# The last FFN's gate and up products in passes of 256 tokens instead of 512

## The reference, cut to what matters

```
h = rmsnorm_2(x, norm_ffn[l])                       # 512 tokens x 1024
x = x + (jax.nn.silu(h @ w_ffn_gate[l])             # 1024 x 2816 weights
         * (h @ w_ffn_up[l])) @ w_ffn_down[l]       # then 2816 x 1024
```

## Time and profile before

| | |
|---|---|
| median of three runs | 1888.11 us |
| profiled execution, span of the core | 1888.1 us |
| mean granted clock of TensorE | 0.998 |
| PE busy | 1859.0 us (98%) |
| PEld (weight loads) busy | 1454.0 us (77%) |
| DVE, ACT, POOL busy | 859.6, 686.3, 552.0 us |
| matmul records | 8653, as many weight loads |

### The profile page before, as it was taken

The page is one execution under the profiler, slowest core; times in us unless marked ns, Lnnn a source line. Parts: engine busy times, 40 slices in busy tenths (PEclk is TensorE's granted clock), DMA queues, the critical chain, the costliest instruction groups (busy, mean ns, idle before and its releaser), DMA issues.

```text
span 1888.1 us, 21529 instructions
## 1 busy us (share of the span) xinstructions
PE 1859.0 (98%) x8653; PEld 1454.0 (77%) x8653; DVE 859.6 (46%) x1348; ACT 686.3 (36%) x1023; POOL 552.0 (29%) x437
## 2 busy tenths in 40 slices
PE   6999999999999999999999999999999999999998
PEld 6777778877777777877888888877776788888886
DVE  6467542646261303324333333548777654423433
ACT  5555542223232323433222222435546532212223
POOL 3543344445355544431000000044556211100100
PEclk9999999999999999999999999999999999999999
DMA  9412223544343122322423322432221222222321
GB/s 300 149 50 68 68 68 123 164 147 155 120 150 110 62 74 85 130 94 87 131 79 100 112 89 70 109 95 79 87 92 58 74 90 93 90 89 91 104 87 54
DMA packets 182332, 192.46 MB, mean 102 GB/s; under 512 B 10155, under 2 KB 166065, under 8 KB 181977
## 3 DMA queue, kind: packets, MB, share of 16 engines
q1 hardware_dynamic: 179704, 180.84, 29.8%
q0 software_dynamic: 1104, 5.24, 1.0%
q10 hardware_dynamic: 1424, 5.00, 0.7%
HBM read 188.95 MB, written 4.72 MB: 103 GB/s over the span
## 4 chain that ended last, share of the span: by engine, by line
PE 93%; DVE 4%; ACT 2%; issue 1%; DMA 0%; ACTq 0%; SPq 0%; DVEq 0%
PE bank L1492 25%; PE bank L1497 24%; PE bank L1494 24%; PE bank L1517 2%; PE bank L1515 2%; PE bank L1513 2%; PE bank L1591 2%; PE bank L1525 2%; PE bank L1541 1%; PE bank L1561 1%; PE bank L1577 1%; DVE left L1859 1%; DVE ADA L1817 1%; PE bank L1471 1%; PE bank L1477 1%
## 5 line engine op out<-in xcount | busy, mean ns | idle before, releaser
L1492 PE MATMUL bank<-hH,wh 128*128 128x512 f32 x1264 | 520.4, 412 | 3.3 <-ACT hH L2221 3.0
L1497 PE MATMUL bank<-hL,wh 128*128 128x512 f32 x1264 | 501.4, 397 | 0.1
L1494 PE MATMUL bank<-hH,wl 128*128 128x512 f32 x1264 | 501.3, 397 | 0.0
L2606 POOL TENSOR_TENSOR wl<-stg,wh 128x512 fp32r<-128x512 f32 x150 | 200.0, 1333 | 792.3 <-ACT wh L2238 792.0
L2238 ACT ACTIVATE wh<-stg 128x1024 fp32r<-128x1024 f32 (+2 forms) x292 | 298.2, 1023 | 271.5 <-PE bank L1497 191.3
L1492 PEld LDWEIGHTS bank<-hH,wh 128*128 128x128 f32 x1264 | 238.4, 189 | 76.0 <-issue 23.3
L1497 PEld LDWEIGHTS bank<-hL,wh 128*128 128x128 f32 x1264 | 238.3, 189 | 58.1 <-DVE hL L1973 0.5
L1494 PEld LDWEIGHTS bank<-hH,wl 128*128 128x128 f32 x1264 | 239.1, 189 | 53.4 <-issue 2.6
L1799 DVE TENSOR_TENSOR wl<-stg,wh 128x1024 fp32r<-128x1024 f32 (+2 forms) x142 | 168.3, 1188 | 240.0 <-ACT wh L2238 239.5
L2607 POOL TENSOR_TENSOR wl<-stg,wh 128x512 fp32r<-128x512 f32 x150 | 203.8, 1359 | 0.0
L1492 PE MATMUL bank<-h2H,wh 128*128 128x512 f32 x352 | 140.6, 399 | 0.0
(11 more groups left out here) (326 smaller groups left out, 2599.8 us busy)
## 6 DMA issues: line engine op xcount, KB each, us to landing
stg<-in_w_in SPq DMA_DIRECT2D x54, 1024.0 KB, 5.1
stg<-in_w_ffn_in SPq DMA_DIRECT2D x22, 1024.0 KB, 5.1
stg<-in_w_ada SPq DMA_DIRECT2D x16, 1024.0 KB, 5.3
stg<-in_w_ffn_gate SPq DMA_DIRECT2D x11, 1024.0 KB, 5.2
stg<-in_w_ffn_up SPq DMA_DIRECT2D x11, 1024.0 KB, 5.1
stg<-in_w_ffn_down SPq DMA_DIRECT2D x10, 1024.0 KB, 5.0
stg<-in_w_ada SPq DMA_DIRECT2D x16, 512.0 KB, 6.4
stg<-in_w_proj_ret SPq DMA_DIRECT2D x8, 1024.0 KB, 5.0
```

Of the source, the lines that this page charges most:

```text
L1492: T.matmul(ps, wh, xh, start=j["first"] and k == 0, stop=False)
L1494: T.matmul(ps, wl, xh, start=False, stop=False)
L1497: t = T.matmul(ps, wh, xl, start=False, stop=j["stop"] and last)
L2606: G.tensor_tensor(lo[:, 0:h, :], src[:, 0:h, :], hi[:, 0:h, :], ALU.subtract)
```

## The change

For jobs whose activations are `h5`, each matmul over 512 tokens becomes two over 256 tokens, one behind the other, with the same weights. The first writes columns 0 to 255 of the bank, the second columns 256 to 511. The flag that starts an accumulation stands on the first half of the first matmul only; later writes accumulate. The semaphore `gemm` is raised by the second half of the last matmul. Jobs with other activations are issued as before.

```
-                T.matmul(ps, wh, xh, start=j["first"] and k == 0, stop=False)
+                last = k == j["n"] - 1
+                halves = [slice(0, S // 2), slice(S // 2, S)] if j["x"] == "h5" else [slice(0, S)]
+                for c in halves:
+                    T.matmul(ps[:, c], wh, xh[:, c], start=j["first"] and k == 0 and c.start == 0, stop=False, skip_group_check=len(halves) > 1)
                 pe.wait_ge("w_lo_" + j["lo"], j["low"])
-                T.matmul(ps, wl, xh, start=False, stop=False)
+                for c in halves:
+                    T.matmul(ps[:, c], wl, xh[:, c], start=False, stop=False, skip_group_check=len(halves) > 1)
                 low_done(pe, j["x"], j["x0"] + k)
-                last = k == j["n"] - 1
-                t = T.matmul(ps, wh, xl, start=False, stop=j["stop"] and last)
+                for c in halves:
+                    t = T.matmul(ps[:, c], wh, xl[:, c], start=False, stop=j["stop"] and last, skip_group_check=len(halves) > 1)
                 if last:
                     t.then_inc(s["gemm"], 1)
```

## The result

The change makes the kernel slower by 0.16%: the ratio to the kernel before is 1.0016, with a 95% interval from 1.0009 to 1.0023, over 17 runs of the kernel after and 16 of the kernel before (medians 1891.95 and 1889.20 us). A 17th run of the kernel before took 3698.86 us, is no fast run and is not in the ratio. The difference is clear of zero. Its middle lies within the 0.2% called no change in the prediction, and the interval's upper end just beyond. The profiled execution has a span of 1891.2 us against 1888.1, so +3.1 us, where +2.6 were forecast; the medians differ by 2.75 us.

A forecast was written before the change was run, and what follows sets the result against it. TensorE was taken to bound the kernel; 1056 pairs, each 2.5 ns dearer than one pass (237.0 against 234.5 ns), add +2.6 us to 1888.1, giving 1890.7 us. Its own range is 1888 to 1896, the wider one 1877 to 1912.

The forecast's parts named there:

- The bound: Last FFN's changed products: TensorE, busy 98% of the span, has 0.0 us idle ahead, so each ns per pass shows 1056 times.
- Twice the loads, all hidden: Each half has its own load, 1056 more in all, ready 112 ns into a 118.5 ns half, 6.5 ns to spare.
- The rival of an uncovered load or issue: Added loads or TensorE's issue of twice the instructions come into the open: up to +116 us, 2004 us; chance 0.07.
- The 21 ns as a rate: A 512-column pass's excess over 213.3 ns grows with columns, 0.453 ns a column, so a half costs 118.5 ns; chance 0.60.
- the rival of a fixed cost: Each fp32r pass keeps its 21 ns at its stream's start: 127.9 ns a half, +22.4 us, 1910.5 us; chance 0.20.
- The rival of short passes that escape: Supply runs dry only late in a stream, so halves go at the load's 112 ns: -11.1 us, 1877.0 us; chance 0.11.
- a supply of columns: In fp32r streams, the supply of columns can't keep up with 2.4 GHz; at half speed the array never waits for it.
- Cost that is there once for each pass: About 2.5 ns for each pass, read from float32 rows; an added pass per pair makes 1056 * 2.5 ns = +2.6 us.
- the sum: For a half pass: 2.5 + 256 * 0.453 = 118.5 ns, a pair 237.0 ns, 2.5 more than one whole pass.
- slower: Outcome beyond the 0.2%, 3.8 us, that a measurement tells from no change; given 0.46 in all.
- The half-clock rows: At granted clock 0.50 passes take 428 ns against 426.7 streamed: the extra is gone, where a cost in array cycles would have doubled.
- The reading that the load in the shadow takes no part of the 21 ns: Behind the pass at 1479.98, 0.227 us of stream runs with no load beside it, so the load isn't the extra's cause.

The follow-up runs named there:

- quarters: Each pass of the last FFN's gate and up products cut into four of 128 tokens, against the kernel before: 2111.64 us, ratio 1.1178.
- even and odd tokens: Changed kernel, but the first half reads even tokens and the second odd ones, 8 bytes apart; results land at wrong tokens: 2121.76 us.
- the run with ones: Kernel before, last FFN's gate and up products all bfloat16, moving operand a dense tile of ones; result left wrong: 1870.52 us.

## Why the prediction was right

The bound: right. TensorE has no idle time ahead of the halves, the stretch starts at the same 1504.2 us, and the difference is inside it.

The time: 1890.7 us were forecast and 1891.95 measured. Most of that gap is in the base and not in the change: a run's time lies 1.8 to 1.9 us above its core's span (1893.07 and 1891.2 us for the profiled run of the kernel after), so the span of 1888.1 and the first three runs' median of 1888.11 were equal by chance, and over more runs the median of the kernel before is 1889.20.

Twice the loads, all hidden: right. The load's pace, 112 ns from float32 rows, held for fp32r (111.7 in quarters), so a half has 6 to 7 ns to spare. The records are 281 to 282 ns long where 280 were forecast. The rival of an uncovered load or issue is out: TensorE was given a pass and a load every 112 ns for all of the last FFN.

The 21 ns as a rate: right in its size and wrong in what it is a rate of. The steps of 118.6 (256), 173.3 to 176.7 (384) and 234.3 (512) deny the rival of a fixed cost, which asked for 127.9 and 181.2. The rival of short passes that escape asked for 112 ns and is out by the same numbers. But "a supply of columns" was too narrow: even and odd tokens show that twice the stretch of memory for the same columns takes nearly twice the time. The prediction couldn't see that, since every moving operand of type fp32r here lies in one piece.

"Cost that is there once for each pass", 2.5 ns: this term came out near by luck, and with it the +2.6 us, which is nothing but this term. It was measured at 3.1 ns a pair in the last FFN, but it isn't a constant of a pass of fp32r: in the first FFN the same halves cost 0.4 ns a pair, and 384 columns lie on both sides of the sum's 176.5. With 117.3 ns a half the change would have cost 0.4 us. The rows didn't give the term either: a step of (1.88 - 0.59) / 3 is known to some 3 ns, and the transposes' 109 to 110 ns are also the pace of their loads, which the prediction itself puts at 110. A cost of 2.5 ns is seen where the array sets the pace (215.8 against 213.3 in the run with ones). What sets the pattern of steps wasn't found.

One bound was worked out wrongly. The prediction lets "slower" begin at about 120.3 ns a half. 3.8 us on 1056 pairs are 3.6 ns a pair, so it begins at (234.5 + 3.6) / 2 = 119.1 ns, 0.6 above the sum, as the prediction has it where it gives the chances. The measured 118.7 lies between the sum and that bound.

The half-clock rows were the reading that carried the choice between rate and fixed cost, and the choice held. The reading that the load in the shadow takes no part of the 21 ns wasn't tested by a run of its own, since every pass has its load; but the bfloat16 pass of 215.8 ns has one in its shadow too (a record of 0.10 us, where those of fp32r have 0.19), and lacks the 18.7 ns.

## What to carry to other kernels

Cutting a pass costs little as long as each part streams longer than a load takes, here 112 ns; below that every part costs 112 ns, and four quarters take nearly twice as long as the whole pass (447 ns against 234). Before cutting, compare the step from pass to pass with columns over clock: what is left over may be the reading of the moving operand, which halves with the memory that a part covers and not with its columns. Keep moving operands dense: every second element of fp32r cost nearly as much time as the full stretch (227 to 229 ns against 234).

## What was not expected of the hardware

- A moving operand that covers 2 KB took 227 to 234 ns in each of the three forms that were run: 512 fp32r in one piece 234.3, 512 bfloat16 4 bytes apart 226.7, 256 fp32r 8 bytes apart 226.7 or 228.9. Dense bfloat16 (1 KB, all ones) went at 215.8 ns for 512 columns.
- The steps between equal passes repeat in short patterns with a fixed mean, and equal passes can have different means in different parts of one kernel, on the same tiles too: 117.3, 118.7 and 120.0 ns for 256 columns, 173.3 and 176.7 for 384. An uninterrupted row keeps its mean.
- A load of bfloat16 weights behind a pass of fp32r started only at the end of that pass's stream, just ahead of its own pass (1600.73 and 1600.74 us, behind 0.26 us of idle time on the loading side); behind a pass of its own type it started with that pass and was hidden (1600.75).
